# Gated DeltaNet stage: first merge of the inverse on 32x32 tiles, key products once per key head, norm weight folded into the output copy, and a new step sequence

## The reference, cut to what matters

```python
def gated_deltanet_mixer(x, w_in, conv_w, a_log, dt_bias, norm_w, w_out):
    proj = x @ w_in                                     # 1024 -> q,k (8 heads), v,z (16 heads), b, a
    qkv = jax.nn.silu(causal_depthwise_conv(qkv, conv_w))
    q, k = l2norm(q), l2norm(k)                         # each key head serves 2 value heads
    beta = sigmoid(b);  g = -exp(a_log) * softplus(a + dt_bias)
    o = chunk_gated_delta_rule(q, k, v, g, beta)
    o = o * lax.rsqrt(mean(o * o) + RMS_EPS) * norm_w   # norm_w: 128 values, one per head column
    o = o * jax.nn.silu(z)
    return o @ w_out

# inside chunk_gated_delta_rule, per value head:
    a = where(strict, (k_beta @ k.T) * decay, 0)        # k @ k.T is the same for the 2 value heads of a key head
    t_inv = triangular_solve(eye + a, eye)              # unit lower triangular inverse
```

## Time and profile before

| | |
|---|---|
| median of 3 runs | 1505.03 us (1503.19 to 1507.46) |
| profiled execution | 1502.73 us, its span 1500.9 us |
| mean granted TensorE clock in it | 0.991 |
| TensorE, matmul / weight load busy | 97% / 79% |
| VectorE / ScalarE / GpSimd busy | 68% / 55% / 5% |
| HBM traffic | 158 GB/s over the span |

### The profile page before, as it was taken

How to read it: one execution, slowest core, us unless ns; L and a number is a source line. 1 busy time by engine, 2 the same in 40 slices (tenths; PEclk the granted TensorE clock), 3 DMA queues, 4 the chain that set the end, 5 groups by cost and what they waited for, 6 DMA issues and landing times.

```text
span 1500.9 us, 19405 instructions
## 1 busy us (share of the span) xinstructions
...
## 2 busy tenths in 40 slices
...
GB/s 204 167 141 104 127 181 140 113 113 174 190 188 180 191 185 168 184 195 189 177 195 182 186 185 191 189 163 145 151 89 95 115 59 113 140 188 191 187 181 109
DMA packets 166274, 238.80 MB, mean 159 GB/s; under 512 B 19406, under 2 KB 112376, under 8 KB 166184
## 3 DMA queue, kind: packets, MB, share of 16 engines
...
HBM read 235.96 MB, written 1.57 MB: 158 GB/s over the span
## 4 chain that ended last, share of the span: by engine, by line
PE 87%; DVE 4%; DMA 3%; ACT 2%; issue 2%; POOL 1%; ACTq 1%; SPq 0%; DVEq 0%; POOLq 0%
PE A L240 16%; PE A L241 15%; PE A L242 15%; PE G L240 5%; PE M L240 5%; PE G L242 5%; PE M L242 5%; PE M L241 5%; PE G L241 5%; PE A L1155 1%; DVE w_lo L224 1%; PE G L1076 1%; DMA raw<-in_ffn_w_gate_up 1%; PE G L1123 1%; DMA raw<-in_gdn_w_in 1%
## 5 line engine op out<-in xcount | busy, mean ns | idle before, releaser
L224 DVE TENSOR_TENSOR w_lo<-raw,w_hi 128x1024 fp32r<-128x1024 f32 (+1 forms) x295 | 506.1, 1738 | 184.3 <-ACT w_hi L206 183.6
L206 ACT ACTIVATE w_hi<-raw 128x1024 fp32r<-128x1024 f32 (+1 forms) x295 | 423.0, 1463 | 196.3 <-DMA raw<-in_ffn_w_gate_up 148.8
L240 PE MATMUL A<-w_hi,x_hi 128*128 128x512 f32 (+1 forms) x640 | 262.8, 411 | 5.8 <-DVE w_lo L224 4.2
L242 PE MATMUL A<-w_hi,x_lo 128*128 128x512 f32 (+1 forms) x640 | 248.4, 388 | 0.0
L241 PE MATMUL A<-w_lo,x_hi 128*128 128x512 f32 (+1 forms) x640 | 248.1, 388 | 0.0
L240 PEld LDWEIGHTS A<-w_hi,x_hi 128*128 128x128 f32 x640 | 121.7, 190 | 36.2 <-DVE x_lo L384 6.4
L242 PEld LDWEIGHTS A<-w_hi,x_lo 128*128 128x128 f32 x640 | 121.2, 189 | 25.4
L240 PE MATMUL A<-w_hi,ffn_ffn_hT_hi 128*128 128x512 f32 x352 | 138.8, 394 | 0.0
L241 PE MATMUL A<-w_lo,ffn_ffn_hT_hi 128*128 128x512 f32 x352 | 138.4, 393 | 0.0
L241 PEld LDWEIGHTS A<-w_lo,x_hi 128*128 128x128 f32 x640 | 121.8, 190 | 20.8 <-issue 1.0
L242 PE MATMUL A<-w_hi,ffn_ffn_hT_lo 128*128 128x512 f32 x352 | 137.4, 390 | 0.0
...
## 6 DMA issues: line engine op xcount, KB each, us to landing
...
```

Source lines behind the costliest of these rows:

```text
L206: ins = act.activation(net.w_hi[:, v % RING, part], net.raw[:, v % RING, part], ACT.Copy)
L224: ins = dve.tensor_tensor(net.w_lo[:, v % RING, part], net.raw[:, v % RING, part], net.w_hi[:, v % RING, part].bitcast(F32), ALU.subtract)
L240: pe.matmul(out, xh, hi[:, k, c, :], start=start and k == 0, stop=False)
L242: mm = pe.matmul(out, xl, hi[:, k, c, :], start=False, stop=stop and k == nk - 1)
```

## The change

1. In `x2` and `t2` the level from 16 to 32 runs on the four 32x32 diagonal tiles of each matrix, at tile positions (0,0), (32,32), (64,64), (96,96): `x2` is 16 products of 32 columns per key head in place of 4 of 128; `t2` is 28 products of 16 columns in place of 8 of 64. ScalarE copies 128x128 elements in `x2` where it copied 128x512. VectorE makes 7 subtractions of 32 partitions by 64 elements in `t2` where it made 2 of 128 partitions by 256.
2. `kk:g:1` no longer computes k kT; `kd:g:1` reads the product of `kk:g:0` in A2. A2 is released by `kd:g:1`, A3 already when VectorE has read the decay (`k_min`).
3. The blocks of `U` that are written in `t1` and `t0` are zero before, so they are written as negated copies by ScalarE (3 small copies per key head) and no longer subtracted by VectorE (3 operations fewer); `x0` waits for VectorE's update of `Tm` alone, `p0` for ScalarE.
4. The norm weight comes as a column with the other columns (one DMA more on ScalarE's queue at the start of the program, one fewer on GpSimd's), and is the scale of the output copy in `ot`; the four multiplications L2625 are gone.
5. `GDN_ORDER` is a new list.

```diff
-    unit:v0:0:1 l2:k1:1 blocks:0 lo:10:0 lo:10:1 lo:11:0 lo:11:1 norm:k1:0
+    unit:q1:1:1 evac:q1:0 blocks:0 lo:9:1 lo:10:0 lo:10:1
...
-        self.rows_dram = (dram["gdn_a_log_2"], dram["gdn_dt_bias_2"], dram["gdn_norm_w_2"])
+        self.rows_dram = (dram["gdn_a_log_2"], dram["gdn_dt_bias_2"])
+        self.norm_w = net.columns(dram["gdn_norm_w_2"])
...
-        sem, per = {"pe": (self.c_pe, 12), "act": (self.c_act, 8), "dve": (self.c_dve, 6),
+        sem, per = {"pe": (self.c_pe, 12), "act": (self.c_act, 10), "dve": (self.c_dve, 5),
...
+        if step[0] == "kk" and step[2] == "1":
+            return "k_min"
...
+            elif by == "k_min":
+                eng.wait_ge(*self.k_min(self.kks.index(before[-1][1:3]) + 1))
...
-                for t in range(TT):
+                for t in range(TT if j == 0 else 0):
...
-                mm = pe.matmul(bg[:, n * P:(n + 1) * P], self.ML[i][:, n, :], self.Tm[i][:, n, :],
-                               start=True, stop=True)
+                for b in range(0, P, 32):
+                    part = slice(b, b + 32)
+                    mm = pe.matmul(bg[part, n * 32:(n + 1) * 32], self.ML[i][part, n, part], self.Tm[i][part, n, part],
+                                   start=True, stop=True, tile_position=(b, b))
...
-                left = self.X[i][:, n, :].rearrange("p (b h r) -> p b h r", h=2, r=16)[:, :, 0, :]
-                pe.matmul(bm[:, n * 64:(n + 1) * 64], self.U[i][:, n, :], left, start=True, stop=True)
-                right = self.U[i][:, n, :].rearrange("p (b h r) -> p b h r", h=2, r=16)[:, :, 1, :]
-                mm = pe.matmul(bm[:, T + n * 64:T + (n + 1) * 64], self.X[i][:, n, :], right,
-                               start=True, stop=True)
+                for b in range(0, P, 32):
+                    part = slice(b, b + 32)
+                    mm = pe.matmul(bm[part, n * 16:(n + 1) * 16], self.X[i][part, n, 0:32],
+                                   self.U[i][part, n, b + 16:b + 32], start=True, stop=True, tile_position=(b, b))
+            for n in range(4):
+                for b in (0, 32, 64):
+                    part = slice(b, b + 32)
+                    mm = pe.matmul(bm[part, 64 + n * 16:64 + (n + 1) * 16], self.U[i][part, n, part],
+                                   self.X[i][part, n, 0:16], start=True, stop=True, tile_position=(b, b))
...
-            pe.wait_ge(*dve(3))
+            pe.wait_ge(*act(6))
...
-                act.activation(self.o_hi[n // 4][:, at:at + 2, :], self.ot_banks[n][:, :], ACT.Copy)\
+                act.activation(self.o_hi[n // 4][:, at:at + 2, :], self.ot_banks[n][:, :], ACT.Copy, scale=self.norm_w)\
...
-            if x == "x2":
-                ins = act.activation(self.X[i][:, :, :], bg[:, :], ACT.Copy)
-            elif x == "x1":
+            if x != "x0":
...
+        elif x == "t1":
+
+            act.wait_ge(*pe(5))
+            for row, col in ((0, 32), (64, 96)):
+                ins = act.activation(self.U[i][row:row + 32, :, col:col + 32],
+                                     bm[row:row + 32, 0:P].rearrange("p (n c) -> p n c", n=4), ACT.Copy, scale=-1.0)
+                if row == 0:
+                    w.chain.mark(ins)
+        elif x == "t0":
+            act.wait_ge(*pe(7))
+            ins = act.activation(self.U[i][0:64, :, 64:P], bm[0:64, 0:T].rearrange("p (n c) -> p n c", n=4),
+                                 ACT.Copy, scale=-1.0)
         elif x == "p0":
             act.wait_ge(*pe(8))
...
-                bank, h = net.A[2 + j], 2 * g + j
+                bank, h = net.A[2], 2 * g + j
...
-                    w.chain(dve.tensor_tensor(u, u, z, ALU.mult))
-                    uh = u.rearrange("p t (h e) -> p (t h) e", e=P)
-                    w.chain.mark(dve.tensor_tensor(uh, uh, self.n_row[:, :].unsqueeze(1)
-                                                   .to_broadcast([P, TT * 4, P]), ALU.mult))
+                    w.chain.mark(dve.tensor_tensor(u, u, z, ALU.mult))
...
-                dve.tensor_tensor(self.o_lo[n // 4][:, at, :], self.ot_banks[n][:, :],
-                                  self.o_hi[n // 4][:, at, :].bitcast(F32), ALU.subtract)\
+                dve.scalar_tensor_tensor(out=self.o_lo[n // 4][:, at, :].rearrange("p k t -> p (k t)"),
+                                         in0=self.ot_banks[n][:, :], scalar=self.norm_w,
+                                         in1=self.o_hi[n // 4][:, at, :].bitcast(F32).rearrange("p k t -> p (k t)"),
+                                         op0=ALU.mult, op1=ALU.subtract)\
...
-        if x[0] == "t":
-            lev = int(x[1])
+        if x == "t2":
             U, Tm = self.U[i], self.Tm[i]
-            dve.wait_ge(*pe(3 + 2 * (2 - lev)))
-            if lev < 2:
-                dve.wait_ge(*own(2 - lev))
-            if lev == 2:
-                for m, right, at in ((Tm, 0, 0), (U, 1, T)):
-                    half = m[:, :, :].rearrange("p n c -> p (n c)")\
-                        .rearrange("p (b h r) -> p b h r", h=2, r=16)[:, :, right, :]
-                    ins = dve.tensor_tensor(half, half, bm[:, at:at + T].rearrange("p (b r) -> p b r", r=16),
-                                            ALU.subtract)
-                    if m is Tm:
-                        w.chain.mark(ins)
-            elif lev == 1:
-                for m, row, col, at in ((Tm, 32, 0, T), (U, 0, 32, 0), (U, 64, 96, 0)):
-                    part = m[row:row + 32, :, col:col + 32]
-                    new = bm[row:row + 32, at:at + P].rearrange("p (n c) -> p n c", n=4)
-                    ins = dve.tensor_tensor(part, part, new, ALU.subtract)
-                    if row < 64:
-                        w.chain.mark(ins)
-            else:
-                part = U[0:64, :, 64:P]
-                ins = dve.tensor_tensor(part, part, bm[0:64, 0:T].rearrange("p (n c) -> p n c", n=4), ALU.subtract)
+            dve.wait_ge(*pe(3))
+            for m, row, col, at in ((Tm, 0, 0, 64), (Tm, 32, 32, 64), (Tm, 64, 64, 64),
+                                    (U, 0, 16, 0), (U, 32, 48, 0), (U, 64, 80, 0), (U, 96, 112, 0)):
+                part = m[row:row + 32, :, col:col + 16]
+                new = bm[row:row + 32, at:at + 64].rearrange("p (n c) -> p n c", n=4)
+                ins = dve.tensor_tensor(part, part, new, ALU.subtract)
+                if row < 96:
+                    w.chain.mark(ins)
             ins.then_inc(sem.sem, 1)
+        elif x == "t1":
+            dve.wait_ge(*pe(5))
+            dve.wait_ge(*own(1))
+            part = self.Tm[i][32:64, :, 0:32]
+            dve.tensor_tensor(part, part, bm[32:64, T:T + P].rearrange("p (n c) -> p n c", n=4), ALU.subtract)\
+               .then_inc(sem.sem, 1)
```

More of the change, by code:

```diff
@@ L1837 @@
-    out:3:1 hi:30:0 hi:30:1 core:7:p4 core:6:p4
-    out:3:2 lo:29:1 ot:4
+    unit:k1:0:3 lo:5:1
+    unit:k1:1:0 ba:t
+    unit:k1:1:1 evac:k1:0 ba:0
+    unit:k1:1:2 lo:6:0 norm:k0:0
+    unit:k1:1:3 evac:k1:1 l2:k0:1 lo:6:1
+    unit:q0:0:0 conv:k1:0
+    unit:q0:0:1 hi:7:0 norm:k0:1
+    unit:q0:0:2 hi:7:1 ba:1
+    unit:q0:0:3 silu:k1:0:0 lo:7:0 kk:0:0 kk:0:1
+    unit:q0:1:0 kd:0:0 lo:7:1 kd:0:1 conv:k1:1 hi:8:0 hi:8:1
+    unit:q0:1:1 evac:q0:0 hi:9:0
+    unit:q0:1:2 kk:1:0
+    unit:q0:1:3 kk:1:1 kd:1:0 evac:q0:1 silu:k1:0:1
@@ new lines @@
+    unit:v0:1:0
+    unit:v0:1:1 silu:q0:1:1 evac:v0:0 lo:12:0
+    unit:v0:1:2
+    unit:v0:1:3 l2:q0:1 lo:12:1 norm:q0:0 norm:q0:1 conv:q1:0 solved:0 evac:v0:1
+    unit:v1:0:0 conv:q1:1 hi:13:0 hi:13:1 hi:14:0
+    unit:v1:0:1 spread:0 silu:q1:0:0
+    unit:v1:0:2
+    unit:v1:0:3 lo:13:0 lo:13:1
+    unit:v1:1:0 kk:4:0
+    unit:v1:1:1 kk:4:1 kd:4:0
+    unit:v1:1:2 evac:v1:0 silu:q1:0:1
+    unit:v1:1:3 kd:4:1 hi:14:1 evac:v1:1 hi:15:0 silu:q1:1:0 lo:14:0 lo:14:1
+    unit:v2:0:0 kk:5:0
+    unit:v2:0:1 kk:5:1 kd:5:0 core:0:k1
@@ new lines @@
+    unit:z0:1:1 conv:v2:0 core:2:k1 core:3:k1 gather:1
+    unit:z0:1:2 conv:v2:1 evac:z0:0 core:2:x2 core:3:x2
+    unit:z0:1:3 hi:20:1 evac:z0:1 hi:21:0
+    unit:z1:0:0 silu:v2:0:0 silu:v2:1:0 core:3:t2
+    unit:z1:0:1 hi:21:1 core:2:t2
+    unit:z1:0:2 core:3:x1
+    unit:z1:0:3 silu:v2:0:1 silu:v2:1:1 vt:v2:0 core:2:x1 vt:v2:1 lo:20:0 lo:20:1 core:3:t1 core:2:t1 lo:21:0
+        lo:21:1 conv:v3:0 solved:1 hi:22:0 core:3:x0
+    unit:z1:1:0 hi:22:1 lo:22:0 lo:22:1 core:2:x0
+    unit:z1:1:1 conv:v3:1 core:3:t0 core:2:t0 evac:z1:0
```

227 lines of the change are left out of this document (98 added, 129 removed).

## The result

The changed kernel takes 1484.97 us (median of 4 runs, 1483.32 to 1486.08), the kernel before 1504.59: a ratio of 0.9864, 95% interval 0.9848 to 0.9881. It is faster, and by 8 us more than forecast; it lies 0.03 us under the low end of the range. The profiled execution took 1486.08 us, its span is 1484.3, the granted clock 0.99 in both.

A forecast was written before the change was run, and what follows sets the result against it. TensorE was taken as the bound of the GDN stage. Terms -8.3, -2.9, +1.1, -1.2, -0.9 and +0.4 sum to -11.8 us: from 1502.7 to 1490.9, with 2.3 for the median 1493 us; range 1485 to 1501.

The forecast's parts named there:

- What a 32x32 product costs: TensorE in `x2` and `t2`: about 21.6 ns a record, so `x2` takes 0.69 us and `t2` 1.21.
- the `t1` row: Profile timing of one `t1`, 24 records in 0.52 us, 0.0217 us each, taken as the price of new tile records.
- My lower end for `t2`: Bound for new `t2` on TensorE if columns count in proportion: 0.61 us, half of 1.21.
- Entries, +1.1: TensorE entering tile steps: 11 new entries in the order, together costing 1.1 us more.
- Rival 3: Four row positions writing one PSUM bank don't overlap: 60 ns a record, 1520 us; chance 0.07.
- Start, -2.9: Stage start: TensorE's evacuation wait and its clock loss shrink to 0.8 us, saving 2.9 us.
- First solve, 8.6 us: TensorE's wait behind the solve 4.4, clock 2.1, short waits for `kd`, `lo`, norm 2.1; before 7.5, so +1.1 us.
- Rival 1: The first solve is hidden, so its 4.4 us wait and 2.1 us clock loss go: 1487 us; chance 0.2.
- Mask, -1.2: TensorE's wait for the mask after `spread` falls from 1.8 to 0.6 us, saving 1.2 us.
- `U`, -0.9: TensorE's waits for VectorE's update of `U`: 0.9 of their 2.3 us go.
- The column load, +0.4: One more DMA issue on ScalarE's queue ahead of the program's first copy costs 0.4 us.
- the tile term: TensorE's saving from tiles in `x2` and `t2`: 0.73 us per key head, 5.8 us over 8 heads.

The follow-up runs named there:

- e7: Changed kernel with about 64 extra, unread tile products ahead of each head's `x2`, to price a record: 32.0 ns at one position, 15.9 at two; no kernel time given.
- e6: Changed kernel with `x2` and `t2` done as before, on whole-array products without tiles: 1493.7 us.
- e10: Changed kernel with the key products made for both heads of a key head again: 1494.5 us.

## Why the prediction was wrong

- **What a 32x32 product costs: the failed step.** "I take the `t1` row" gave 21.7 ns a record, the `x1` row beside it 21.6. Both rows ran to the start of the next product, so they held the way out of the tiles; by its group `x1` is (0.69 - 0.2) / 31 = 15.8 ns, what two positions in turn cost in e7, and a third of `t1`'s records go to one position, the dearest case. `x2` and `t2` take four or three in turn, 8.4 and 10.4 ns. `x2` and `t2` fell by 13 us, not 5.8. My lower end for `t2`, 0.61 us if columns counted in proportion, was about what it took, by luck: from 32 to 16 columns nothing changes, positions count; and `x2` had no lower end at all.
- **Entries, +1.1:** e6 against the changed kernel gives some 2. Right in kind.
- **Rival 3, and the Trainium skill beside it.** The Trainium skill (TensorEngine Tiling (Array Packing), Gotcha 1: PSUM Pressure) has different row tiles unable to access a bank at once. Four row positions in turn wrote one bank, each to its own 32 partitions, at 8.4 ns a record; the trace shows no such cost. The Trainium skill's overhead of about 60 cycles a matmul (TensorEngine Tiling (Array Packing), Instruction Overhead), as an estimate 25 ns at 2.4 GHz, is near the 31 ns of one position and three times too high for four.
- **Start, -2.9:** right, it was -3.2. The wait of 1.98 and 1.7 of lost clock became one wait of 0.52 us, for the evacuation of `ba`, at full clock.
- **First solve, 8.6 us:** the wait was 5.0 (4.4 forecast), `kd`, norm and `lo` 2.0 (0.45, 1.12 and 0.40; 2.1 forecast), the clock behind it 3.0 (2.1 forecast). Right in kind, 1.4 us low in all. Rival 1, a hidden solve, had 1487 us, near the measured time, and is not what happened.
- **Mask, -1.2:** the wait of 1.8 went whole.
- **`U`, -0.9:** right as a count of waits of before (2.3 to none), wrong as a price. The sequence leans on it, 9.4 us.
- **The end of the stage: missed.** Before, TensorE waited 3.57 us for `w_lo` (from 1290.40 on) and ran at 0.85 for the 11.16 us behind; after, 2.43 and 1.00 over 9.66. That is 2.8 us that I had no term for: the stage ran to 1305, and my rows ended at 1285 to 1290. The other way, four waits of 0.7 to 0.9 us behind the first core step are new, 3.0 us in all, one of them "issue".
- **The column load, +0.4:** not seen above a spread of 2 us in that spot.

The terms as measured: tiles -13.1, entries +2, key products -3.3 (e10), TensorE's idle time 15.6 to 13.0 so -2.6, clock 5.5 to 3.0 so -2.6. That makes -19.6 against a stage 18.4 us shorter; 1.2 us I can't assign. So the miss is the tile term: -11.8 was forecast, and 7.3 of the 7.8 us beyond it are its size, while the smaller errors about cancel.

My sum treated the parts as independent, and they are not: each part of the code taken back alone costs 8.7, 9.4, 9.5 and 2.8 us, 30 in all for a change worth 19.6, and the sequence taken back costs 31; added to the kernel before, the sequence alone costs 4, the code alone 11.
